# Experts' weights in tiles of 2048 columns, five buffers for high parts with a lead of four tiles, and column halves only at the end of the last expert's second matrix

## The reference, cut to what matters

```
def _swiglu(h, w_gate_up, w_down):
    gu = h @ w_gate_up
    g, u = gu[..., :D_FF], gu[..., D_FF:]
    return (jax.nn.silu(g) * u) @ w_down

for e in range(N_EXPERTS):
    y = y + gate_full[..., e:e + 1] * _swiglu(h, w_gate_up[e], w_down[e])
x = x + y
```

## Time and profile before

| | |
|---|---|
| median of 3 runs | 1522.73 us (1520.2 to 1609.3) |
| the profiled execution, its time and its span | 1522.17 us, 1520.2 us |
| PE, PE loads, DVE, ACT, POOL busy | 97%, 80%, 76%, 65%, 9% of the span |
| DMA | 468.26 MB, mean 308 GB/s |
| the experts' stage | from about 617 us to 1509 us |

### The profile page before, as it was taken

The page is one execution under the profiler, slowest core; times in us unless marked ns, Lnnn a source line. Parts: engine busy times, 40 slices in busy tenths (PEclk is TensorE's granted clock), DMA queues, the critical chain, the costliest instruction groups (busy, mean ns, idle before and its releaser), DMA issues.

```text
span 1520.2 us, 19543 instructions
## 1 busy us (share of the span) xinstructions
PE 1481.3 (97%) x7678; PEld 1208.7 (80%) x7678; DVE 1158.3 (76%) x1021; ACT 991.1 (65%) x869; POOL 132.2 (9%) x137
## 2 busy tenths in 40 slices
PE   8999999999989999999999999999999999999996
PEld 6888888899969987888777788777888777888774
DVE  5555445454565456899899988899898999898997
ACT  5544434343453337777798777888776888776986
POOL 0000000006034314000000200000100000000000
PEclk9999999999999999999999999999999999999999
DMA  9655555567516653899999999999999999999996
GB/s 333 214 170 190 168 192 171 189 192 224 194 57 213 206 185 126 329 356 355 366 405 417 398 407 405 395 408 415 399 408 403 395 408 415 399 404 408 393 391 220
DMA packets 151056, 468.26 MB, mean 308 GB/s; under 512 B 9856, under 2 KB 15872, under 8 KB 138416
## 3 DMA queue, kind: packets, MB, share of 16 engines
q1 hardware_dynamic: 144784, 453.93, 79.8%
q0 software_dynamic: 2816, 9.96, 2.3%
q10 hardware_dynamic: 3360, 3.06, 0.7%
HBM read 459.55 MB, written 7.37 MB: 307 GB/s over the span
## 4 chain that ended last, share of the span: by engine, by line
PE 79%; DVE 13%; ACT 3%; DMA 1%; SPq 1%; issue 1%; DVEq 0%; ACTq 0%
DVE wlo L418 9%; PE bS L437 6%; PE bS L438 6%; PE bS L436 6%; PE bY L436 6%; PE bY L438 6%; PE bY L437 6%; PE bG L436 4%; PE bG L438 4%; PE bU L436 4%; PE bG L437 4%; PE bU L438 4%; PE bU L437 4%; DVE wlo_more L418 2%; ACT whi L412 2%
## 5 line engine op out<-in xcount | busy, mean ns | idle before, releaser
L418 DVE TENSOR_TENSOR wlo<-raw,whi 128x2048 fp32r<-128x2048 f32 x364 | 827.2, 2296 | 179.6 <-ACT whi L412 178.4
L412 ACT ACTIVATE whi<-raw 128x2048 fp32r<-128x2048 f32 x364 | 692.3, 1915 | 262.1 <-PE bS L438 118.2
L418 DVE TENSOR_TENSOR wlo_more<-raw_more,whi 128x2048 fp32r<-128x2048 f32 x60 | 136.4, 2288 | 10.7 <-ACT whi L412 10.6
L412 ACT ACTIVATE whi<-raw_more 128x2048 fp32r<-128x2048 f32 x60 | 114.5, 1914 | 28.0 <-DMA raw_more<-in_m_w_gate_up_dram 8.4
L1086 PE MATMUL bY<-whi,hTh 128*128 128x512 f32 x224 | 91.5, 408 | 6.9 <-DVE wlo L418 4.9
L436 PE MATMUL bY<-whi,hTh 128*128 128x512 f32 x224 | 89.8, 401 | 0.0
L437 PE MATMUL bY<-whi,hTl 128*128 128x512 f32 x224 | 89.1, 398 | 0.0
L437 PE MATMUL bS<-whi,eTl 128*128 128x512 f32 x192 | 76.4, 398 | 0.0
L436 PE MATMUL bS<-whi,eTh 128*128 128x512 f32 x192 | 76.4, 398 | 0.0
L1086 PE MATMUL bS<-whi,eTh 128*128 128x512 f32 x192 | 76.3, 398 | 0.0
L1087 PE MATMUL bY<-wlo,hTh 128*128 128x512 f32 x184 | 73.2, 398 | 0.0
(11 more groups left out here) (536 smaller groups left out, 3336.4 us busy)
## 6 DMA issues: line engine op xcount, KB each, us to landing
raw<-in_m_w_gate_up_dram SPq DMA_DIRECT2D x184, 1024.0 KB, 14.5
raw<-in_m_w_down_dram SPq DMA_DIRECT2D x90, 1024.0 KB, 14.4
raw_more<-in_m_w_gate_up_dram SPq DMA_DIRECT2D x40, 1024.0 KB, 14.6
raw<-in_b_w_in_dram SPq DMA_DIRECT2D x36, 1024.0 KB, 5.1
raw<-in_f_w_gate_up_dram SPq DMA_DIRECT2D x28, 1024.0 KB, 5.2
raw_more<-in_m_w_down_dram SPq DMA_DIRECT2D x20, 1024.0 KB, 14.2
raw<-in_f_w_down_dram SPq DMA_DIRECT2D x14, 1024.0 KB, 5.0
raw<-in_a_w_out_dram SPq DMA_DIRECT2D x4, 1024.0 KB, 16.8
```

Source lines behind the costliest of these rows:

```text
L412: nc.scalar.activation(whi[:, h], raw_of(r), ACT.Copy).then_inc(hi_done, 1)
L418: nc.vector.tensor_tensor(wlo_of(r), raw_of(r), whi[:, h].bitcast(F32), ALU.subtract).then_inc(lo_done, 1)
```

## The change

The first matrix is cut into groups of 2048 columns: a tile holds 128 rows x 2048 columns in pieces of 8 KB, eight tiles make a group, and its four slabs go to G, S0, S1 and U at the same time. Three groups hold gate 0 to 3, gate 4 to 6 with up 0, and up 1 to 4; up 5 and 6 are left for four tiles of 256 rows x 1024 columns in pieces of 4 KB. A new semaphore `gu_psum` tells when each of the first three banks of a group is complete; the first tile of the next group waits for each bank as it comes to it. The gate results of all seven slabs lie in `parked` (in the place of `hTl`, which is not filled until later), the up results in `mbuf` and `mbuf_odd`, four deep. The turns move to tiles 17, 24, 25, 27, 29, 31 and 33. A fifth buffer for high parts, `whi_late`, lies where `hn` was, and is used from tile 6 of item 0 on; ACT and DVE work four tiles ahead (LEAD), and SP loads four tiles of the next expert before it goes on. In item 7 the first six tiles of the second matrix are like those of the other items and the other eight hold 512 rows x 512 columns, four for each half; Y0 is complete after tile 37, and `spread_left` stands behind tile 40, before the last.

```diff
 HI = 4
 CUT = 3
+LEAD = 4
...
-PAIRS = SLABS // 2
-SINGLE = 8 * PAIRS
+GROUPS = 2 * FF // 2048
+NARROW = KD * GROUPS
+LAST_WIDE = 6
+LAST_HALF = 4
+UPS_OF = ((), (0,), (1, 2, 3, 4), (5, 6))
...
+            if t < NARROW:
+                g, kb = divmod(t, KD)
+                return gate_up[kb * P:kb * P + P, g * 2048:g * 2048 + 2048]
             if t < DOWN:
+                q = t - NARROW
+                return gate_up[q * 256:q * 256 + 256, GROUPS * 2048:2 * FF].rearrange("(k p) n -> p k n", p=P)
+            if by_half and t >= DOWN + LAST_WIDE:
+                h, qn = divmod(t - DOWN - LAST_WIDE, LAST_HALF)
+                r = LAST_WIDE * 256 + qn * 512
+                return down[r:r + 512, h * 512:h * 512 + 512].rearrange("(k p) n -> p k n", p=P)
...
+        T_LATE = -(-(T_MOE + HI + 1) // HI) * HI
+        def hi_slot(t):
+            return t % HI if t < T_LATE else (0, HI, 1, 2, 3)[(t - T_LATE) % (HI + 1)]
...
+        gate_up_banks = G, S0, S1, U
+        def column_sums(engine, n, g, s):
+            if s == (3 if g < GROUPS else 1):
+                engine.wait_ge(tile_used, count(n, FFN_TILES, T_MOE + (KD * g + KD if g < GROUPS else DOWN)))
+            else:
+                engine.wait_ge(gu_psum, count(n, 10, 3 * g + s + 1))
...
+                def bank_free(g, s):
+                    if g == 1:
+                        pe.wait_ge(silu_done, count(k, SLABS, PAIRS0 + s + 1))
+                    if g == 2 and s < 3:
+                        pe.wait_ge(silu_done, count(k, SLABS, PAIRS0 + s + 5))
+                    if g == 2 and s == 3:
+                        pe.wait_ge(h_ready, count(k, SLABS, PAIRS0 + 1))
+                    if g == 3:
+                        pe.wait_ge(h_ready, count(k, SLABS, PAIRS0 + s + 2))
...
+                turns = {17: 0, 24: 1, 25: 2, 27: 3, 29: 4, 31: 5, 33: 6}
+                for t in range(DOWN):
+                    gate_up_product(t)
+                    if t in turns:
+                        turn(turns[t])
+                    if t in (3, 11, 25):
+                        amid(t // KD)
...
-                    if t == DOWN + (10 if by_half else 5):
+                    if t == DOWN + (12 if by_half else 5):
                         late()
...
+                turned = {18: 0, 25: 1, 26: 2, 28: 3, 30: 4, 32: 5, 34: 6}
+                for t in range(FFN_TILES):
+                    ahead(t)
+                    if t in (3, 11):
+                        amid(t // KD)
+                    if t in (7, 15):
+                        for j in range(4) if t == 7 else range(4, SLABS):
+                            silu(j)
+                    if t in turned:
+                        hidden_hi(turned[t])
...
+                turned = {18: 0, 25: 1, 26: 2, 28: 3, 30: 4, 32: 5, 34: 6}
+                for t in range(FFN_TILES):
+                    ahead(t)
+                    if t in (14, 22, 27):
+                        muls({14: 1, 22: 2, 27: 3}[t])
+                    if t in turned:
+                        hidden_lo(turned[t])
...
+                    if t in (7, 15):
+                        for j in range(4) if t == 7 else range(4, SLABS):
+                            copy_gate(j)
+                    if t in (15, 23, 27):
+                        copy_ups((t - 7) // KD if t < 27 else 3)
...
+                    if by_half and t == DOWN + 9:
+                        y_cut(0)
```

More of the change, by code:

```diff
@@ L410, in make_hi @@
             if t >= HI:
-                act.wait_ge(tile_used, used_count(t, item, HI))
-            nc.scalar.activation(whi[:, h], raw_of(r), ACT.Copy).then_inc(hi_done, 1)
+                act.wait_ge(tile_used, hi_free(t, item))
+            if isinstance(item, int) and in_order(t, item) == T_LATE + 1:
+                act.wait_ge(hn_out, 32)
+                act.wait_ge(gd_psum, 4)
+            nc.scalar.activation(whi_of(h), raw_of(r), ACT.Copy).then_inc(hi_done, 1)
         def make_lo(dve, t, item=0):
@@ L431, in wblk_backward @@
                 wlo_more, (r - RAW) * 2048 + b * 512, MORE * 2048)
-            return backward(whi, h * 2048 + b * 512, HI * 2048), low
+            high = backward(whi, h * 2048 + b * 512, HI * 2048) if h < HI else backward(whi_late, b * 512, 2048)
+            return high, low
         def mm3(pe, dst, a, b, start, stop):
@@ new lines, in full_item @@
+                for t in range(DOWN):
[4 more added lines that the diff above has]
+                        amid(t // KD)
+                before_down()
+                for t in range(DOWN, FFN_TILES):
+                    pe.wait_ge(ht_lo, count(k, SLABS, PAIRS0 + (t - DOWN) // 2 + 1))
+                    down_product(t)
+                    if t in turns:
+                        turn(turns[t])
+                    if t == DOWN + 5:
@@ new lines, in gate_up_product @@
+                def gate_up_product(t):
+                    tile_ready(T_MOE + t, n)
+                    for s, blk, kb, stop in blocks_of(t, False):
+                        if t < KD:
+                            tokens_ready(n, kb, s)
+                        if kb == 0:
+                            bank_free(t // KD, s)
+                        w = wblk_backward(T_MOE + t, blk, n)
+                        pe.matmul(backward(gate_up_banks[s], 0, 512), eTh[:, kb], w[0], start=kb == 0, stop=False)
+                        mm = pe.matmul(backward(gate_up_banks[s], 0, 512), eTh[:, kb], w[1], start=False, stop=stop)
+                        if stop and s < (3 if t < NARROW else 1):
+                            mm.then_inc(gu_psum, 1)
+                    mm.then_inc(tile_used, 1)
```

431 lines of the change are left out of this document (153 added, 278 removed).

## The result

The changed kernel takes 1533.05 us (median of 6 runs, 1530.89 to 1535.74), the kernel before 1523.78 beside it: ratio 1.0065, 95% interval 1.0046 to 1.0084. It is slower by 9 us where 6.5 less were forecast. The profiled execution took 1530.9 us, its span is 1529.0.

A forecast was written before the change was run, and what follows sets the result against it. PE, DVE and DMA were all near their limit, the chain alternating PE and DVE, with DMA only in the last expert. Terms +1.0, -4.4, +0.2 and -3.3 sum to -6.5 from 1522.17: 1516 us, range 1507 to 1530.

The forecast's parts named there:

- in half items the slip of some 0.3 is PE's slack of 0.33 a tile: Bank boundaries in half items: ACT's slightly late release of banks is absorbed by PE's slack, so nothing was charged.
- the forecast's 51.4: Half items: DVE reaches tile 24's low part 51.4 us after the item's start; PE then needs 46.1.
- 97.7: Forecast length in us of a half item after the change, a gain of 2.5 each.
- rival C: ACT's in-order queue comes late to every bank boundary and PE waits: 1539 to 1549 us, chance 0.17.
- the sign that was to tell of C: Profile after: full items growing by over 1 us would show ACT late at bank boundaries.
- The lead: Fifth high buffer and working four tiles ahead: one low part fewer after the switch, 2.5 us gained per half item.
- The pair of 217.8: DMA time for a full plus a half item, down from 222.4 and under the engines' 220.2, so not binding.
- 2.8 us for it: Item 2: tile 8 needs tile 11 landed, so PE stalls 2.8 us, once only.
- The 8 KB pieces: Wider pieces of the first matrix save 0.07 us a tile on 24 tiles, 1.7 per expert.
- The last expert: Item 7: wider second-matrix pieces take DMA out of the chain, and its last matmul ends 3.3 us earlier.
- The 98.5: Last expert: PE's last matmul ends 98.5 us after the item's start, against 101.8 before.
- a bound of the second part: Lead of four: no gain, half items staying at 100.2 us, if bunched turns throttle PE more.

The follow-up runs named there:

- half items mended: Changed kernel, full loads; in half items banks emptied ahead of the high part of tile t+4 or earlier, slab 0 split three tiles later: 1532.01 us, ratio 1.0062.
- both orders mended: Half-item order mended, plus full-item SiLUs that empty banks put ahead of the high part of tile t+4, on the changed kernel: 1518.08 us, 0.9969 to the kernel before.
- copies first on halved loads: Changed kernel, half-item banks emptied before tile t+4's high part; first 24 tiles per expert from the second load only 1024 columns: 1521.52 us, ratio 0.9999.
- copies first on full loads: Changed kernel with ACT, in half items, emptying a group's four banks before making the high part of tile t+4: 1527.76 us, 1.0042 to the kernel before.
- 4 KB pieces: Changed kernel with full- and half-item orders mended, first matrix's first 24 tiles loaded in 4 KB instead of 8 KB pieces: 1525.99 us, 1.0027 to the kernel before.

## Why the prediction was wrong, point by point

**The step that failed** is, in the part on groups of four banks, "in half items the slip of some 0.3 is PE's slack of 0.33 a tile". It priced ACT's copy as if every high part ahead of it were on time. In half items they were not: in item 3 those of tiles 17 to 19 and of 26 and 27 wait for landings, and where landings are early, ACT waits for DVE's multiplication of slab 0. Tile 24 so starts 3.7 to 4.3 later than the forecast's 51.4, and 46 us of PE work follow whatever happens, 47.6 where the clock falls. That is 3.4, 4.1 and 5.5 us over 97.7 in items 1, 3 and 5. Shown by undoing it: without landings and with slab 0 later, half items take 97.4, and on full loads with the whole order mended 97.6 to 98.0. It is rival C's mechanism, "ACT is one copy behind", with a chance of 0.17. I had priced it mostly in full items, where ACT has time; there it did not show in the changed kernel (122.2), so the sign that was to tell of C, full items over 1 us longer, stayed out while its mechanism made nearly all of the loss.

**The lead** was right for DVE alone: 2.5 a half item forecast, 3.9 measured with loads out of the way. With full loads it brought 2.1 in the first half item and cost 0.3 in the next two and 3.4 in the last. The forecast let the shorter DMAs make room for it.

**The pair of 217.8** was the wrong measure. DMA's mean over a pair says nothing about when a tile lands. In the second half of a full item the ring is full and SP waits for slots (50 of the 62 us up to item 3), so the faster DMA saves nothing there; what counts is how soon tile 11 of the next full item lands after that, and with half items at 97.8 it lands 3.4 too late for PE. The forecast had the mechanism and 2.8 us for it, and then let it go after one pair because it "gains 2.4 per pair on the engines"; the run with half items mended shows it in all three. In the changed kernel itself it did not occur because its half items were too long.

**The 8 KB pieces** were right: 0.07 us a tile (2.56 to 2.49), forecast 0.07. The Trainium skill (DMA: Bandwidth & Descriptors, section Why small descriptors are slow) has a fixed cost of about 3 cycles a packet, by which an estimate gives 1.2%, less than half of this 2.7%; the rows decide.

**The last expert**: -3.3 forecast, +3.3 measured. The part alone brings 0, with the 2 KB pieces at the end still 2.70 apart. In the changed kernel that the DMA "drops out" holds for this end: none of its last fourteen high parts waits for a landing, and 47.2 follow tile 24, near the 47.7 forecast. But tile 24 is at 57.5 instead of 50.8, and the chain runs to it through a DMA after all, that of tile 19, and through the copy for tile 16 behind it, where PE idles 4.68 and the clock is at 0.50 for 7 us:

```profile
1430.97 15.20 DMA raw<-in_m_w_gate_up_dram
1446.22 1.79 issue
1448.01 0.59 ACT parked L1256
```

The 98.5 is met only without landings (98.7); with both orders mended on full loads this item takes 102.9, longer than before (101.4).

**The clock** was in no term of the sum, only in a bound of the second part. It fell in each half item behind the waits; behind tile 24 of item 5 it cost 1.6 (47.6 against 46.05).

**The range** of 1507 to 1530 missed by 3. C began at 1539, and nothing was laid between its mild form and that.

## What to carry to other kernels

An engine with one queue both prefetches and frees banks here: before moving a release, list what stands ahead of it in that queue and the worst time at which each of these can start, a landing and another engine included, and put the release ahead of the prefetch. A faster DMA was worth something here only while its ring had free slots, so price it by the landing of the tile that someone waits for next, not by its mean. When one stretch is made faster, look for the first wait behind it that had been hidden by its length: mending half items alone put 15 us into the full ones.

## What the runs showed of the hardware

TensorE's granted clock fell to its lower level, 0.50 (1.2 GHz), for some 3 us, in places 7 or 10, behind waits of PE in an otherwise full stage. The length of the one wait does not tell when. With copies first on halved loads, PE idles 2.09, 2.08 and 2.09 us before tile 24 of items 1, 3 and 5, and the clock fell behind the first two and not behind the third. In the changed kernel it fell behind 2.30 us (tile 24 of item 5) and not behind 2.48 (item 3); with copies first on full loads behind 2.71 and not behind 2.78; with 4 KB pieces behind a last wait of 1.3. Where PE is what sets the end, a stretch of 3 us costs 1.3 to 1.6 us, one of 10 us 4.1; ten spare matmuls in the wait took that away in full items (127.1 to 125.7). Where PE has to wait again anyway it costs nothing, and filling the first wait can move the fall to a worse place: 6 to 8 us more.
